# Sparse attention in a hybrid RWKV-7 and S5 model: top-256 keys by a bit search for the threshold, index scores computed one unit earlier, ties by a prefix sum

## The chip, the cores and the metric

The kernel runs on one core of a Trainium2 chip. A core has five engines with a queue each: PE (TensorE, matrix products), DVE (VectorE), ACT (ScalarE), POOL (GpSimd) and SP (SyncE, which here issues the DMAs). They run in parallel and wait for each other through semaphores. The metric is the device time of one execution in microseconds (us), the median of several runs.

## The reference

One program computes two blocks one after the other. The first is an RWKV-7 mixer and a short convolution; the change doesn't touch it. The second is a hybrid layer: an S5 state space branch with a gated unit, and a sparse attention. Only this part matters here:

```python
def block(args):                         # 128 queries at a time, 8 blocks
    blk, ql_b, qi_b, wi_b = args
    causal = key_pos[None, :] <= q_pos[:, None]
    idx_logits = jnp.einsum('bthd,bsd->bths', qi_b, ki)          # 8 index heads of 32
    index_score = jnp.einsum('bths,bth->bts', jax.nn.relu(idx_logits), wi_b)
    index_score = jnp.where(causal[None], index_score, neg)
    _, sel = lax.top_k(index_score, n_sel)                       # n_sel = 256 of 1024 keys
    ...
    s = jnp.einsum('bthc,btkc->bthk', ql_b, c_sel)               # 8 heads over a latent of 128
    s = jnp.where(valid[:, :, None, :], s, neg)
    p = jax.nn.softmax(s, axis=-1)
    return jnp.einsum('bthk,btkc->bthc', p, c_sel)
```

`top_k` takes, among equal scores, those with the lower index. The gated unit is `y = gelu(y); h = y @ w_glu + b_glu; val * sigmoid(gate)`, multiplied by `silu(gate_s)`, whose product with `w_in` is also made in that unit.

## The kernel before

All data are float32. After the first block, the second runs as four units, with a barrier of all engines at the end of each: the S5 scan with projections (lines 1486 to 1827), the gated unit (lines 1829 to 1944), attention (`attention_block`, line 1947) and the output product with layer norm (line 2290).

**The gated unit** has two loops. The first has 8 steps (j, `SUB`): GELU of 512 columns on ACT and DVE, four transposes on PE, a copy to `yT` on DVE (L1931), and beside it 8 matrix products of the gate (L1860) a step. The second has 4 steps (e, `NE`): 32 products of PE (L1889), two tanh on ACT, and five operations of DVE over 1024 columns (L1935 to L1943); PE's gate products for e+2 wait for DVE's L1940 (`out2`), and follow between the steps.

**Attention, preparation** (L1981 to L2058): index weights `wi` by a transpose, `kiT` (the index keys four times below each other) by four DMAs, `ql` and the latent `cT`. DVE ends with the gate's sigmoid (L2056, L2058), four times.

**Attention, main loop.** 8 blocks b of 128 queries, in each 8 heads h; a slot k is 8b+h. Block b sees `keys(b)` = 128(b+1) keys. In a slot PE makes the scores for slot k+2 (L2094), the transposes of the softmax (L2111), the values (L2119) and one product by `w_uv` (L2130); DVE adds the mask and takes the maximum (`softmax`, L2245 and L2248) and inverts the sum (L2266); ACT makes the exponentials and copies out of PSUM. Blocks 0 and 1 see at most 256 keys and need no choice.

Blocks 2 to 7 do. Before, in slots 0 to 47, PE also makes one head's index logits two blocks ahead (L2102), ACT takes the ReLU and the weight (L2185, L2194), POOL sums over heads (L2210) and DVE chooses for block b+1 in slots h = 1 to 7 of block b (`choose`): 32 rounds of the 8 largest by `max` (L2257) and their removal by `match_replace` (L2258), in place in `score`, then the mask `mb` (L2260).

```python
for i in range((h - 1) * steps // parts, h * steps // parts):
    ch(nc.vector.max(top[:, :], sc))
    ch(nc.vector.match_replace(sc, top[:, :], sc, LEAST))
```

`ch` makes DVE wait for its own last instruction. The order within each engine is written out by hand, nothing is scheduled by a tool.

## Time and profile before

| | |
|---|---|
| median of 3 runs | 4590.96 us (4587.19 to 4592.53) |
| the profiled execution's own time | 4586.48 us |
| its span, first to last instruction | 4584.8 us |
| busy: PE, DVE, ACT, POOL | 4219.0, 2370.4, 1315.9, 274.1 us |
| gated unit, first loop | from 3697 to 3749 us |
| gated unit, second loop | to 3857 us |
| attention, preparation | to 3889 us |
| attention, main loop | to 4442 us |
| output unit | to the end |

The stages follow one another in time. A share over the whole span says little on the change: what counts is which engine others wait for in the stages from 3697 to 4442 us.

### The profile page before, as it was taken

The page shows a single profiled execution, that of the slowest core. Times are in us where ns is not written, and L with a number is a line of the kernel's source. Part 1 is how long each engine was busy: PE and PEld are TensorE (multiplying, and loading weights), DVE is VectorE, ACT ScalarE, POOL GpSimd, SP SyncE. Part 2 cuts the span into 40 slices and gives each one's busy share as a digit, 9 for nine tenths or more (in the row PEclk, how much of TensorE's full clock was granted, in tenths as well). Part 3 has the DMA queues.
Part 4 walks back from the last instruction along what each step waited for, and adds up shares of the span by engine and source line. Part 5 has one row for each costly group of instructions (what it writes and reads, how often), then busy time and mean ns, then how long its engine had stood idle before and what let it go on. Part 6 is the DMA issues. An engine that isn't in the chain of part 4 may idle for free. (4 is left out here: it accounts for less than half of the span.)

```text
span 4584.8 us, 131580 instructions
## 1 busy us (share of the span) xinstructions
PE 4219.0 (92%) x58346; PEld 3217.2 (70%) x58346; DVE 2370.4 (52%) x5302; ACT 1315.9 (29%) x3044; POOL 274.1 (6%) x308
## 2 busy tenths in 40 slices
PE   7999999999999999998988999999969977877579
PEld 5888888888888888886777887888746643444344
DVE  4556555565555655554215543444255533688842
ACT  2233323332323223222213332232113312433221
POOL 1000000000000000000000000000000000111100
PEclk9999999999999999998999999999989988566789
DMA  2322222222222222221413333333211110000010
GB/s 74 92 68 79 63 88 68 83 64 78 77 79 68 79 68 77 70 79 50 127 37 110 96 96 83 101 96 96 55 42 28 23 37 9 1 1 0 0 46 37
DMA packets 520412, 289.54 MB, mean 63 GB/s; under 512 B 30256, under 2 KB 509728, under 8 KB 519904
## 3 DMA queue, kind: packets, MB, share of 16 engines
q1 hardware_dynamic: 519904, 281.88, 21.3%
q8 instruction: 427, 7.00, 0.6%
q14 instruction: 81, 0.66, 0.0%
HBM read 267.55 MB, written 12.58 MB: 61 GB/s over the span
## 5 line engine op out<-in xcount | busy, mean ns | idle before, releaser
L344 PE MATMUL a_bank<-a_lerps,a_wt 128*128 128x256 f32 x4096 | 1036.9, 393 | 2.4 <-DVE a_lerps L815 2.4
L344 PEld LDWEIGHTS a_bank<-a_lerps,a_wt 128*128 128x128 f32 x4096 | 731.0, 189 | 126.9 <-issue 21.2
L1208 PE MATMUL b_bank<-b_hR,b_wR 128*128 128x512 f32 x1024 | 399.8, 390 | 15.5 <-DVE b_wL L1213 15.5
L1208 PE MATMUL b_bank<-b_hL,b_wR 128*128 128x512 f32 x1024 | 399.7, 390 | 0.0
L1208 PE MATMUL b_bank<-b_hR,b_wL 128*128 128x512 f32 x1024 | 399.5, 390 | 0.0
L931 DVE TENSOR_TENSOR a_iv_X<-a_bank,a_iv_X 128x256 f32<-128x256 f32 x256 | 108.7, 425 | 413.3 <-PE a_bank L448 413.3
L1213 DVE TENSOR_TENSOR b_wL<-b_w,b_wR 128x1024 fp32r<-128x1024 f32 (+1 forms) x144 | 192.4, 1340 | 116.8 <-ACT b_wR L1296 104.0
L692 ACT ACTIVATE a_iv<-a_bank 128x512 f32<-128x512 f32 x192 | 114.7, 597 | 419.1 <-PE a_bank L454 266.2
L1208 PEld LDWEIGHTS b_bank<-b_hR,b_wR 128*128 128x128 f32 x1024 | 193.0, 188 | 56.0 <-issue 16.1
L1208 PEld LDWEIGHTS b_bank<-b_hL,b_wR 128*128 128x128 f32 x1024 | 192.9, 188 | 40.4
L1208 PEld LDWEIGHTS b_bank<-b_hR,b_wL 128*128 128x128 f32 x1024 | 193.0, 189 | 40.2
L1701 PE MATMUL s_proj<-xT,s_wp 128*128 128x512 f32 x384 | 172.3, 599 | 11.9 <-DMA s_wp<-in_w_in 11.9
L448 PEld LDWEIGHTS a_bank<-a_iv 32*32 32x32 f32 x12288 | 130.0, 105 | 70.1 <-issue 69.6
L2257 DVE MAX8 tb_top<-tb_score 128x8 f32<-128x384 f32 (+5 forms) x192 | 171.2, 892 | 5.2
L1008 DVE SCALAR_TENSOR_TENSOR a_S<-a_bank,a_scr,a_pr_H 128x64 f32<-128x64 f32 x256 | 72.5, 283 | 189.2 <-PE a_bank L568 189.2
L2258 DVE MATCH_REPLACE8 tb_score<-tb_top,tb_score 128x384 f32<-128x384 f32 (+5 forms) x192 | 168.1, 875 | 0.0
L1296 ACT ACTIVATE b_wR<-b_w 128x1024 fp32r<-128x1024 f32 x128 | 134.1, 1052 | 109.7 <-issue 90.5
L448 PE MATMUL a_bank<-a_iv 32*32 32x32 f32 x12288 | 157.5, 194 | 2.9 <-issue 2.7
L752 POOL TENSOR_TENSOR a_scr<-a_scr 128x256 f32<-128x256 f32 x64 | 46.5, 726 | 1760.3 <-ACT a_scr L658 1744.0
L2130 PE MATMUL t_po<-t_wuv,tb_oT 128*128 128x64 f32 x128 | 37.9, 394 | 107.8 <-ACT tb_oT L2191 101.5
L2119 PEld LDWEIGHTS t_po<-tb_pT,t_ck 128*128 128x128 f32 x576 | 97.6, 254 | 52.6 <-issue 49.2
L1701 PEld LDWEIGHTS s_proj<-xT,s_wp 128*128 128x128 f32 x384 | 71.3, 192 | 89.6 <-issue 89.6
(441 smaller groups left out, 8156.7 us busy)
## 6 DMA issues: line engine op xcount, KB each, us to landing
a_wt<-in_a_w_in SPq DMA_DIRECT2D x256, 512.0 KB, 4.2
b_w<-in_b_w_in SPq DMA_DIRECT2D x128, 512.0 KB, 4.0
b_w<-in_b_w_out SPq DMA_DIRECT2D x16, 1024.0 KB, 5.6
rwkv_out<-a_ybuf SPq DMA_DIRECT2D x64, 128.0 KB, 5.7
m_w<-in_a_w_out SPq DMA_DIRECT2D x16, 512.0 KB, 4.0
s_wp<-in_w_in SPq DMA_DIRECT2D x12, 512.0 KB, 3.8
a_xtok<-in_x SPq DMA_DIRECT2D x4, 1024.0 KB, 7.1
m_two<-rwkv_out SPq DMA_DIRECT2D x16, 256.0 KB, 3.0
```

The costliest lines, as they stand in the source:

```text
L344: r = mm(o, wt[:, j, c, :], src[:, c, :], start=(c == 0), stop=(c == ND - 1))
L448: r = mm(bank[bk][rows, at + c * CH:at + (c + 1) * CH][:, cols], lhs[rows, c, cols], rhs[rows, c, cols], start=True, stop=True)
L692: return a(tiles[:, :, :, :].rearrange("p w a b -> p (w a b)"), bank[bk][:, :], ACT.Copy, scale=scale).then_inc(s[done], 1)
L931: tt(x, bank[3][:, 0:PASS], x, ALU.add).then_inc(s[after], 1)
L1008: stt(S4[:, c + 1, :], bank[7][:, c * CH:(c + 1) * CH], e["eL"][:, (c + 1) * CH - 1:(c + 1) * CH], pr["H"][:, c, :], ALU.mult, ALU.add).th ...
L1208: m = nc.tensor.matmul(o, a, b, start=(first and i == 0), stop=(last and i == 2))
L1213: return eng.tensor_tensor(l, x, rounded.bitcast(F32), ALU.subtract)
L1296: nc.scalar.activation(wR[:, i, :, :], w[:, i, :, :], ACT.Copy).then_inc(s[f"wR{i}"], 1)
L1701: m = nc.tensor.matmul(proj[:, t], wp[i][:, c, :], xT[:, c, t], start=(c == 0), stop=(c == ND - 1))
L2119: m = nc.tensor.matmul(po[0][:, 0:P], ck[:, j, :], pT[k % 2][:, j * P:(j + 1) * P], start=(j == 0), stop=(j == k // AH))
L2257: ch(nc.vector.max(top[:, :], sc))
L2258: ch(nc.vector.match_replace(sc, top[:, :], sc, LEAST))
```

## The change

It has three parts.

1. **The index scores move.** `kiT`, `wi` and the logits are made in the first loop of the gated unit. The scores of blocks 2 to 7 are cut into 80 pieces (a block of up to 512 keys is one piece a head, the others two halves), 10 a step. For a piece PE makes one product, ACT the ReLU out of PSUM into one of four buffers, and DVE multiplies by the weight and adds (`weigh`), where ACT scaled and POOL added before. PSUM holds two pieces. POOL only applies the causal mask.
2. **The search.** A threshold for each query is found bit by bit: for each of 32 bits, count the scores of at least the candidate (`tensor_scalar` with a sum as second output), and set or clear the bit by two operations on 128x2 integers. Two blocks go through a bit together: group 0 is blocks 2 and 3 (384 and 512 keys), group 1 is 4 and 5 (640, 768), group 2 is 6 and 7 (896, 1024). Where the bits stand is a table:

```python
BITS_BEFORE = 8
BITS_AFTER = ([(0, i) for i in range(8, 23)], [(0, i) for i in range(23, 32)] + [(1, i) for i in range(0, 4)], [(1, i) for i in range(4, 10)], [])
BITS_PRELIM = range(10, 16)
BITS_1 = range(16, 32)
SLOT_2 = 12
```

So 8 bits stand between the gated unit's loops, 15, 13 and 6 after its steps e = 0, 1, 2, 6 of group 1 in the attention's preparation, the other 16 of group 1 one a slot in slots 0 to 15, and the 32 of group 2 one a slot in slots 12 to 43.
3. **The choice.** In slots h = 4, 5, 6 of block b, `choose(b+1)` counts what lies above the threshold, marks the equals, numbers them by a prefix sum, and keeps as many as there is room.

```diff
+    def bit(self, v, g, i):
+        if self.updated:
+            v.wait_ge(s["thr"], self.updated)
+        for b in GROUPS[g]:
+            if self.counted >= 2:
+                v.wait_ge(s["count"], self.counted - 1)
+            nc.vector.tensor_scalar(self.junk[self.counted % 2][:, 0:keys(b)], score_of(sel, b), sel["thr"][:, col].bitcast(F32), None,
+                                    ALU.is_ge, ALU.add, accum_out=sel["cnt"][:, col]).then_inc(s["count"], 1)
+            self.counted += 1
+        v.wait_ge(s["count"], self.counted)
+        place = 31 - i
+        nc.vector.tensor_scalar(sel["flip"][:, cols], sel["cnt"][:, cols], TOPK - 0.5, -1.0 if i == 0 else 2.0 ** place, ALU.is_lt, ALU.mult).then_inc(s["flip"], 1)
+        v.wait_ge(s["flip"], self.updated)
+        nc.vector.scalar_tensor_tensor(sel["thr"][:, cols], sel["flip"][:, cols], (1 << 30) if i == 0 else (1 << place) >> 1, sel["thr"][:, cols],
+                                       ALU.bitwise_xor, ALU.bitwise_xor).then_inc(s["thr"], 1)
...
                     for j in range(SUB):
+                        for n in range(j * PER, (j + 1) * PER):
+                            logits(n)
                         pe.wait_ge(s["gelu"], j + 1)
...
+                    def weigh(n):
+                        v.wait_ge(s["rl"], n + 1)
+                        if h == 0:
+                            ts(o, x, w, None, ALU.mult).then_inc(s["acc"], 1)
+                        else:
+                            v.wait_ge(s["acc"], before)
+                            stt(o, x, w, o, ALU.mult, ALU.add).then_inc(s["acc"], 1)
...
                     def choose(b, h):
-                        steps, parts = TOPK // 8, AH - 1
-                        for i in range((h - 1) * steps // parts, h * steps // parts):
-                            ch(nc.vector.max(top[:, :], sc))
-                            ch(nc.vector.match_replace(sc, top[:, :], sc, LEAST))
+                        if h == AH - 4:
+                            ch(ts(up, sc, t, None, ALU.is_gt, ALU.add, accum_out=above[:, i:i + 1]))
+                            ts(room[:, i:i + 1], above[:, i:i + 1], -UNIT, TOPK * UNIT, ALU.mult, ALU.add)
+                            ch(ts(eq, sc, t, UNIT, ALU.is_equal, ALU.mult))
+                        if h == AH - 3:
+                            ch(nc.vector.tensor_tensor_scan(up, eq, eq, 0.0, ALU.add, ALU.bypass))
+                            ch(stt(eq, up, room[:, i:i + 1], eq, ALU.is_le, ALU.mult))
+                        if h == AH - 2:
+                            ch(ts(out, sc, t, -UNIT, ALU.is_le, ALU.mult))
+                            ch(tt(out, out, eq, ALU.add))
...
-                        if k < ISLOTS:
-                            index(k)
```

In the gated unit, PE's first loop now reads as follows for its first two steps: `g_kiT` against `latent` are the index logits, `s_y` the transposes, `g_ws` the gate.

```order
L1944 MATMUL g_bank<-base_ident,latent 128x128 x8
L1952 MATMUL g_bank<-g_kiT,latent 128x384 x8
L1952 MATMUL g_bank<-g_kiT,latent 128x512 x2
L1964 MATMUL g_bank<-base_ident,s_y 128x128 x4
L1937 MATMUL g_bank<-xT,g_ws 128x512 x4
L1952 MATMUL g_bank<-g_kiT,latent 128x512 x6
L1952 MATMUL g_bank<-g_kiT,latent 128x320 x4
L1964 MATMUL g_bank<-base_ident,s_y 128x128 x4
L1937 MATMUL g_bank<-xT,g_ws 128x512 x4
```

The rows L1944 and L1952 are new there; before, transposes and gate products only alternated. On DVE the second step of the same loop reads now (`sel_score` holds the scores, `g_rl` the ReLU's buffers):

```order
L2049 TENSOR_SCALAR g_g<-g_g 128x512
L2050 TENSOR_TENSOR g_g<-g_g,s_y 128x512
L2043 SCALAR_TENSOR_TENSOR sel_score<-g_rl,g_wi,sel_score 128x512 x5
L2054 TENSOR_SCALAR g_g<-g_g 128x512
L2055 TENSOR_TENSOR s_y<-s_y,g_g 128x512
L2043 SCALAR_TENSOR_TENSOR sel_score<-g_rl,g_wi,sel_score 128x512
L2039 TENSOR_SCALAR sel_score<-g_rl,g_wi 128x320 x2
L2043 SCALAR_TENSOR_TENSOR sel_score<-g_rl,g_wi,sel_score 128x320 x2
L2059 COPY g_yT<-g_bank 128x512
```

Ten operations, L2043 and L2039, stand between the five that a step had before. In the attention loop, one slot of block 4 on DVE before, from one reciprocal to the next (ISA is the masked maximum and its read-out):

```order
L2266 RECIPROCAL tb_den<-tb_den 128x1
L2245 ISA tb_sm,tb_mx<-t_big,tb_mb 128x640
L2245 ISA tb_mx 128x1
L2248 TENSOR_SCALAR tb_nmx<-tb_mx 128x1
L2257 MAX tb_top<-tb_score 128x8
L2258 MATCH_REPLACE tb_score<-tb_top,tb_score 128x768
L2257 MAX tb_top<-tb_score 128x8
L2258 MATCH_REPLACE tb_score<-tb_top,tb_score 128x768
```

and so on for four or five pairs. The same block in the changed kernel, a slot with h = 5 (`sel_thr` the threshold, `tb_same` the equals):

```order
L2345 RECIPROCAL tb_den<-tb_den 128x1
L2319 ISA tb_sm,tb_mx<-t_big,tb_mb 128x640
L2319 ISA tb_mx 128x1
L2322 TENSOR_SCALAR tb_nmx<-tb_mx 128x1
L1524 TENSOR_SCALAR t_junk,sel_cnt<-sel_score,sel_thr 128x896
L1524 TENSOR_SCALAR t_junk,sel_cnt<-sel_score,sel_thr 128x1024
L1531 TENSOR_SCALAR sel_flip<-sel_cnt 128x2
L1533 SCALAR_TENSOR_TENSOR sel_thr<-sel_flip,sel_thr 128x2
L2336 SCALAR_TENSOR_TENSOR tb_upto<-tb_same 128x768
L2337 SCALAR_TENSOR_TENSOR tb_same<-tb_upto,tb_room,tb_same 128x768
```

The pairs are gone; one bit of group 2 (L1524 to L1533) stands in the slot, and here a third of the choice (L2336, the prefix sum, and L2337).

## Rows read from the trace of the kernel before

**Rows 1.** Windows: a piece of the gated unit's first loop; attention loop; blocks 2, 4, 6, 7

```profile
core 0: us, PE busy (x) PEld busy (x) DVE busy (x) ACT busy (x) POOL busy (x), PEclk, DMA share, GB/s
...
3720.00:3748.00 28.00, 24.58 (x73) 10.98 (x72) 17.95 (x28) 5.83 (x11) 0.00 (x0) 1.00 0.00 1
...
3889.00:4442.00 553.00, 409.28 (x1376) 252.98 (x1376) 425.74 (x846) 188.95 (x416) 77.80 (x58) 0.65 0.00 1
...
3984.00:4046.00 62.00, 51.96 (x129) 29.76 (x128) 54.07 (x130) 21.41 (x52) 11.78 (x9) 0.50 0.00 1
...
4125.00:4211.00 86.00, 64.80 (x214) 40.08 (x213) 73.39 (x130) 30.81 (x58) 15.82 (x9) 0.68 0.00 0
...
4305.00:4402.00 97.00, 46.51 (x197) 33.38 (x196) 91.34 (x127) 16.99 (x36) 0.00 (x0) 0.72 0.00 0
...
4409.00:4442.00 33.00, 29.64 (x200) 24.05 (x200) 8.04 (x25) 16.80 (x34) 0.00 (x0) 1.00 0.00 1
```

**Rows 2.** Groups of instructions, whole run: the old search, count | busy us, mean ns | idle before

```profile
L2257 DVE MAX8 tb_top<-tb_score 128x8 f32<-128x384 f32 (+5 forms) x192 | 171.2, 892 | 5.2
...
L2258 DVE MATCH_REPLACE8 tb_score<-tb_top,tb_score 128x384 f32<-128x384 f32 (+5 forms) x192 | 168.1, 875 | 0.0
```

**Rows 3.** Timeline of DVE, one slot of block 4: start us, us

```profile
4155.75 0.16 DVE L2266 RECIPROCAL tb_den<-tb_den 128x1 f32<-128x1 f32 x1
...
4156.95 0.15 DVE L2248 TENSOR_SCALAR tb_nmx<-tb_mx 128x1 f32<-128x1 f32 x1
...
4157.02 0.95 DVE L2257 MAX8 tb_top<-tb_score 128x8 f32<-128x768 f32 x1
...
4167.26 0.16 DVE L2266 RECIPROCAL tb_den<-tb_den 128x1 f32<-128x1 f32 x1
```

**Rows 4.** Groups by shape, DVE, whole run: mean ns of one

```profile
L2361 DVE TENSOR_SCALAR o_r<-o_r,o_st 128x1024 f32<-128x1024 f32 x8 | 6.5, 812 | 0.3
...
L2260 DVE TENSOR_SCALAR tb_mb<-tb_score 128x1024 f32<-128x1024 f32 x1 | 0.7, 693 | 0.0
...
L2260 DVE TENSOR_SCALAR tb_mb<-tb_score 128x384 f32<-128x384 f32 x1 | 0.4, 359 | 0.0
...
L2245 DVE CUSTOM_DVE_ANT_0 tb_sm<-t_big,tb_mb 128x1024 f32<-128x1024 f32 x8 | 9.8, 1225 | 20.1 <-PE t_big L2094 19.9 <-DVE tb_den L2266 0.2
...
L826 DVE TENSOR_TENSOR_SCAN a_scr<-a_const_chunk_keep,a_scr 128x256 f32<-128x256 f32 x64 | 44.3, 692 | 2.2
...
L1384 DVE TENSOR_SCALAR b_tap<-b_cols 128x3 f32 x30 | 35.0, 1165 | 0.0
...
L2052 DVE SCALAR_TENSOR_TENSOR t_cT<-latent,tp_kvg,tp_rs 128x1024 f32<-128x1024 f32 x1 | 1.3, 1285 | 0.0
```

**Rows 5.** Timeline, one step of the gated unit's first loop

```profile
3740.67 1.08 DVE L1931 COPY g_yT<-g_bank 128x512 f32<-128x512 f32 x1 [0.75 <-PE g_bank L1871]
...
3745.13 3.60 PE L1860 MATMUL g_bank<-xT,g_ws 128*128 128x512 f32 x8
...
3745.33 1.08 DVE L1931 COPY g_yT<-g_bank 128x512 f32<-128x512 f32 x1 [0.75 <-PE g_bank L1871]
```

**Rows 6.** Timeline of DVE, second loop of the gated unit, with idle before

```profile
3763.64 0.69 DVE L1935 TENSOR_SCALAR g_th<-g_th 128x1024 f32<-128x1024 f32 x1 [17.23 <-ACT g_th L1908]
...
3799.46 0.69 DVE L1935 TENSOR_SCALAR g_th<-g_th 128x1024 f32<-128x1024 f32 x1 [30.69 <-ACT g_th L1908]
...
3834.45 0.69 DVE L1935 TENSOR_SCALAR g_th<-g_th 128x1024 f32<-128x1024 f32 x1 [29.85 <-ACT g_th L1908]
...
3851.70 0.69 DVE L1935 TENSOR_SCALAR g_th<-g_th 128x1024 f32<-128x1024 f32 x1 [12.12 <-ACT g_th L1908]
```

**Rows 7.** Timeline of DVE, the attention unit's preparation

```profile
3881.25 0.69 DVE L2056 TENSOR_SCALAR tp_gt<-tp_gt 128x1024 f32<-128x1024 f32 x1 [5.61 <-ACT tp_gt L2035]
```

**Rows 8.** Timeline of PE, block 7: transposes of two slots in a row

```profile
4417.85 1.04 PE L2111 MATMUL t_tp<-base_ident,tb_sm 128*128 128x128 f32 x8
...
4422.45 1.04 PE L2111 MATMUL t_tp<-base_ident,tb_sm 128*128 128x128 f32 x8
```

More of the change, by code:

```diff
@@ L1845, in s5_block, with halves, last_piece @@
             sg = sb("sg", [P, SEQ])
+            kiT = sb("kiT", [P, SEQ])
+            wi = sb("wi", [P, NB, IH])
+            rl = sb("rl", [P, 4, HALF])
+            qiT = latent[:, 1:3, :]
+            def halves(b):
+                parts = 1 if keys(b) <= HALF else 2
+                return [slice(i * keys(b) // parts, (i + 1) * keys(b) // parts) for i in range(parts)]
+            pieces = [(b, h, t) for b in range(B0, NB) for h in range(IH) for t in halves(b)]
+            PER = len(pieces) // SUB
+            def last_piece(b):
+                return max(n for n, piece in enumerate(pieces) if piece[0] == b)
             with nc.Block() as block:
@@ L1960, in attention_block @@
         NQ = AH * AD // P
-        qT, qiT = mixed[:, 0:NQ, :], latent[:, 1:3, :]
-        kiT = sb("kiT", [P, SEQ])
-        wi = sb("wi", [P, NB, IH])
+        qT = mixed[:, 0:NQ, :]
+        junk = [sb(f"junk{i}", [P, SEQ]) for i in range(2)]
+        search = Search(nc, s, sel, junk)
         cT = sb("cT", [P, SEQ])
@@ L2065, in sb3 @@
                 return sub.enter_context(nc.sbuf_tensor("tb_" + name, shape, dt))
-            rl = [sb3(f"rl{i}", [P, SEQ]) for i in range(2)]
-            score = [sb3(f"score{i}", [P, SEQ]) for i in range(2)]
-            top = sb3("top", [P, 8])
+            same, upto = sb3("same", [P, SEQ]), sb3("upto", [P, SEQ])
+            above, room = sb3("above", [P, NI]), sb3("room", [P, NI])
             mb = [sb3(f"mb{i}", [P, SEQ]) for i in range(2)]
@@ L2095, in scores @@
                         m.then_inc(s["sc"], 1)
-                    def index(k):
-                        b, h = divmod(k, IH)
-                        pe.wait_ge(s["pT"], k + 1)
-                        rows = slice((h % 4) * IDIM, (h % 4 + 1) * IDIM)
-                        for t in pieces(keys(b + B0)):
-                            m = nc.tensor.matmul(tp[:, t], qiT[rows, h // 4, (b + B0) * P:(b + B0 + 1) * P], kiT[rows, t], start=True, stop=True)
-                        m.then_inc(s["logit"], 1)
                     def turn(k):
```

167 lines of the change are left out of this document (100 added, 67 removed).

## The prediction

> **What bounds the kernel now.** The page shows PE busy for most of the span, but that is the RWKV and convolution part, which stays as it is. I cut the rest into its stages by the timeline and read the windows. In the attention loop DVE is busy 425.7 of 553 us, in block 4 it is 73.4 of 86 us and in block 6 91.3 of 97, while PE's granted clock averages 0.65 over the loop and 0.50 in block 2 [rows 1]. The groups name DVE's work: MAX8 and MATCH_REPLACE8, 192 of each, 171.2 and 168.1 us [rows 2]. The timeline of one slot shows it as a chain: from the reciprocal at 4155.75 the softmax part takes until 4157.02, that is 1.27 us, and the next reciprocal comes at 4167.26, a slot of 11.5 us, filled with five pairs without gaps [rows 3]. Block 7 has no choice to make and shows the loop without it: PE's transposes come 4.60 us apart [rows 8], at a granted clock of 1.0 and with PE 29.6 of 33 us busy [rows 1]. So the loop is bound by DVE in blocks 1 to 6 and by PE in block 7. In the gated unit's first loop a step is 4.66 us, from copy to copy [rows 5], PE is busy 24.6 of 28 us and DVE 17.95 [rows 1], thus DVE has 3.0 us of work in each step, 3.2 with its gaps. In the second loop DVE waits 17.2, 30.7, 29.9 and 12.1 us ahead of its four steps [rows 6]; that is cover, of nearly 90 us.
>
> **The price of the new operations.** Times of DVE go by two rates. A `tensor_scalar` over SBUF takes 693 ns for 1024 elements and 359 ns for 384, that is 0.52 ns an element over some 0.16 us; one with two column operands takes 812 ns. The masked maximum, which also writes out an accumulated value, takes 1225 ns for 1024, or 1.04 ns an element [rows 4]. No row shows a `tensor_scalar` that also sums. Its bounds are therefore 0.69 and 1.23 us for 1024, and as a far one 2.08 ns an element, the prefix sum's rate (692 ns for 256, less 0.16) [rows 4]. I take 1.04 ns an element, because the operation nearest in what it does, an elementwise operation with an accumulator read out behind it, has that rate. A column operand adds 0.06 us (1285 against 1225 ns) [rows 4], an accumulator's read-out with its gap about 0.05. A 128x1 operation takes 0.15 us [rows 3], with its gap 0.19. So one bit, two counts and two small operations, costs:
> group 0 (384, 512 keys): 0.56 + 0.69 + 0.12 + 0.10 + 0.39 = 1.86 us;
> group 1 (640, 768): 0.83 + 0.96 + 0.61 = 2.39 us;
> group 2 (896, 1024): 1.09 + 1.23 + 0.61 = 2.93 us.
> All 96 bits are 230 us, against 339 for the pairs, and 42 of them now stand in DVE's waits of the second loop.
>
> The Trainium skill, "VectorE: DVE Perf Modes", section "The perf-mode tier table (the rule you actually need)", gives `tensor_scalar` in fp32 two elements a cycle in SBUF and doesn't say what an accumulator changes. The 693 ns row agrees for the plain form. By that rule for the counts as well, the case "half-priced counts" below would hold.
>
> **First loop of the gated unit: +43 us.** DVE gets 80 pieces, 33.8 thousand elements in all (8 heads times 4224 keys). At 1.04 ns they are 35.2 us, with 80 times 0.22 us fixed 52.8; the 10 first ones of each head's kind run at the fast rate, -2.2; and 80 gaps of 0.04 make 3.2: 53.8 us. With the 8 steps of 3.2 us this is 79 us of DVE, 9.9 a step, so DVE becomes the bound, not PE (per step 3.6 for the gate's 8 instructions, and for ten products, at the same 0.45 us for 512 columns and 422 columns on the mean, 3.7 [rows 5]). The start costs about 5 us: eight transposes, `wi`, four DMAs of `kiT`, a first product and ReLU come ahead of the first piece; PE's old wait for the DMA of `ws` goes under it. Between a step's last product and the next step's first stand transposes and gate, some 4 us of PE at full clock, with some 5 us of DVE work as cover (pieces still in the buffers, copy, first GELU part). That is near, and I allow 1 us a step, 8 in all. Sum 92 us, against 49: +43. Bounds: +35 with no such stall, and at half clock the gate takes 3.6 us more a step, 29 in all, which gives +72. POOL's last mask (0.3 us) and a semaphore come behind.
>
> **Second loop: +3 us.** The 8 bits take 14.9 us with 0.8 ahead of them, in a wait of 17.2 us which the last pieces shorten: about 1 us late. After e = 0, 15 bits are 27.9 of 30.7 us. After e = 1, 9 and 4 bits are 26.3 of 29.9. After e = 2, 6 bits of group 1 are 14.3 against 12.1 [rows 6]: 2 us late. What is late then is DVE's L1935, which holds the unit's end.
>
> **Attention, preparation: +9 us.** 6 bits, 14.3 us, stand ahead of DVE's gate operations, which waited 5.6 us for ACT's tanh [rows 7]. ACT's tanh and PE's start of the main loop are held by them. The transposes, DMAs and scaling that left this unit lay beside the wait for `w_uk` and the reciprocal, and give nothing.
>
> **Main loop: -245 us.** Index products, ReLU, scaling and POOL's sums leave it. DVE's slot is 1.27 us at 640 keys [rows 3], so 0.60 + 1.04 n, n in thousands of keys: 0.73 in block 0 to 1.67 in block 7. `choose` is 6.25 n + 1.5 (two operations at the fast rate, three at 1.04, the prefix sum at 2.08 ns): 4.0 us for block 2, 8.0 for block 7. PE's slot is 4.6 us at full clock in block 7 and taken in proportion to b + 1, twice that at half clock. The blocks:
> 0: 8 times (0.73 + 2.39) = 25. 1: 7 + 0.7 (the gated product) + 4 slots of one bit, 9.6, + 4 of both groups, 21.3, + 4 = 42.5. 2: 8 + 0.7 + 23.4 + 4.8 = 37, with PE 28 at half clock: 38. 3: 38.7, PE 37 at half clock: 41. 4: 40.7, but PE 46 at half clock and 23 at full: 46. 5: four slots with bits, 11.2 + 0.7 + 11.7 + 7.2 = 31; PE 28 or 55: 39. 6: DVE 21, PE 32 at full clock, and the slots h = 4 and 5 of DVE are longer than PE's: 37. 7: 38. With 2 us at the start 308, against 553.
> I take full clock in blocks 6 and 7, because block 7 before has it as soon as no choice holds its PE, and a mixture in 4 and 5. Blocks 0 to 3 are DVE's at either clock.
>
> **Sum.** 43 + 3 + 9 - 245 = -190 us. From the profiled execution's 4586.48 that is 4396, from the median, which is 4.5 us above it, **4401 us**.
>
> **The rivals.**
> *Half-priced counts.* The sum comes at no cost and the counts run at 0.52 ns an element. Bits are then 1.48, 1.74 and 2.0 us with column operands at the higher price. The second loop is not late (3 less), the preparation is +5 (4 less), and the main loop 20, 33, 31, 36, 42, 36, 37, 38 = 273 (35 less): 4359 us. For it speaks the 693 ns row; against it that every row with an accumulator on DVE has the other rate.
> *PE stays at half clock.* Before, it did in blocks 0 to 2 with PE 52 of 62 us busy [rows 1]. If so to the end, the blocks are 25, 43, 38, 41, 48, 55, 64, 74 = 388, 80 more, and the gated unit's gate 29 more: 4510 us. Against it stands block 7.
> *The small operations are dear.* This one ends on the other side. L1384, three elements in a `tensor_scalar`, takes 1165 ns [rows 4] where others of its size take 150; it has a variable address and I see no other reason. The 192 operations on 128x2 integers are of a kind that no row shows. At 1165 ns each they would add 194 us, with little cover left, and give 4595. From 0.99 us each on the change loses.
> *Slow counts*, at the prefix sum's rate: 32 times 4224 elements times 1.04 ns, +141 less some 10 of cover: 4530 us.
> *The scores' part costs more than it gives:* a stall at each piece (PSUM holds two) would add 0.3 us to each of 80 pieces, +24, 4425; it lies in the range.
>
> **How the numbers follow.** Forecast 0.60, half-priced counts 0.25, half clock 0.06, small operations 0.03, slow counts 0.03, others 0.03. The first two have their middles at 4401 and 4359; to both go the first loop's bounds (-8, +29), and the clock in blocks 4 to 6 (-15 at full, +45 at half, seldom all). So 4345 to 4460; the forecast's own range is 4380 to 4460. A measurement of this kernel tells a change of 0.2%, 9 us. Faster 0.95, within it 0.01, slower 0.04 (the small operations and part of the others).
>
> **What would show it.** Counts of 1024 keys at 1.2 to 1.3 us (or 0.7 to 0.85 for the rival); a gated first loop of some 92 us with DVE busy over 85%; `thr` operations at 0.15 to 0.2 us; in blocks 1 to 4 slots that end on DVE, at 4.6 to 5.3 us; blocks 6 and 7 at clock 1.0 with slots near 4 to 5 us; an attention loop of about 308 us. I am wrong if the first loop is beyond 120 us, or if the clock in blocks 6 and 7 is near 0.5.

## The result and the profile after

The kernel after takes 4417.38 us (median of 4 runs, 4416.63 to 4417.93), the kernel before in the same session 4589.07 us (4 runs, 4586.53 to 4592.53). The ratio is 0.9625, with a 95% interval from 0.9609 to 0.9642: 3.75% faster. The forecast was 4401 us with a range from 4345 to 4460. The sum was off by 16 us, and two of its terms by more than that, in opposite directions: the good total is in part luck.

The stages, cut at the same places in both traces: the gated unit's first DMA and scaling, the first product of its second loop, its last product into `mixed`, attention's first masked maximum, the last gated product. Times are in us.

| stage | before | after | change | forecast |
|---|---|---|---|---|
| up to the gated unit (not touched) | 3697.0 | 3702.5 | +5.5 | 0 |
| gated unit, first loop | 51.6 | 136.9 | +85.3 | +43 |
| gated unit, second loop | 107.0 | 108.3 | +1.3 | +3 |
| attention, preparation | 34.4 | 41.8 | +7.4 | +9 |
| attention, main loop | 551.8 | 283.4 | -268.4 | -245 |
| output | 143.0 | 143.2 | +0.2 | 0 |

The first row is a difference in parts that are the same in both. It differs by this much from run to run: the experiments below, in which these parts are the same too, start the gated unit between 3693 and 3701 us. So stages are compared below by their own length.

The windows of the kernel after answer to [rows 1]: the whole first loop, four pieces of it within two steps, and attention's blocks 1 to 7.

```profile
core 0: us, PE busy (x) PEld busy (x) DVE busy (x) ACT busy (x) POOL busy (x), PEclk, DMA share, GB/s
3702.00:3840.00 138.00, 132.38 (x267) 55.43 (x268) 77.73 (x137) 52.05 (x98) 1.76 (x6) 0.69 0.10 35
...
3756.00:3762.00 6.00, 6.00 (x17) 2.25 (x15) 2.84 (x6) 3.24 (x7) 0.29 (x1) 1.00 0.00 0
3763.00:3768.00 5.00, 5.00 (x11) 2.17 (x10) 3.65 (x7) 1.99 (x4) 0.00 (x0) 0.50 0.00 0
3769.00:3775.00 6.00, 6.00 (x16) 2.37 (x15) 1.94 (x4) 1.96 (x4) 0.00 (x0) 1.00 0.00 0
3776.00:3785.00 9.00, 9.00 (x16) 4.17 (x17) 6.11 (x11) 3.21 (x7) 0.29 (x1) 0.50 0.00 0
...
4018.00:4060.00 42.00, 23.41 (x88) 18.30 (x88) 38.20 (x114) 11.12 (x39) 0.00 (x0) 0.63 0.00 1
4060.00:4096.00 36.00, 24.13 (x112) 17.90 (x112) 33.13 (x90) 13.15 (x41) 0.00 (x0) 0.81 0.00 1
4096.00:4133.00 37.00, 27.03 (x142) 20.29 (x142) 34.72 (x90) 14.35 (x41) 0.00 (x0) 0.86 0.00 1
4133.00:4172.00 39.00, 30.53 (x176) 24.11 (x176) 36.30 (x89) 15.91 (x40) 0.00 (x0) 0.91 0.00 1
4172.00:4205.00 33.00, 30.63 (x201) 24.82 (x200) 25.72 (x60) 18.80 (x42) 0.00 (x0) 1.00 0.01 1
4205.00:4240.00 35.00, 34.19 (x224) 27.39 (x224) 19.28 (x42) 19.84 (x41) 0.00 (x0) 1.00 0.00 1
4240.00:4273.00 33.00, 29.64 (x200) 24.05 (x200) 8.03 (x25) 16.86 (x34) 0.00 (x0) 1.00 0.00 1
```

Two things are to be seen. In the first loop it is PE that is busy, 132.4 of 138 us, and DVE only 77.7; I had forecast the reverse. Its clock averages 0.69 there, and the mean hides two levels: within one step it is 1.0, then 0.50, then 1.0 again, with PE busy throughout. In the attention loop DVE is nearly full in blocks 1 to 4 and PE in 5 to 7, and the clock is at 0.81 as early as block 2, where before it was at 0.50 [rows 1].

The chain of work in one step of the first loop, by the timeline of the kernel after (PE, ACT and DVE):

```profile
3756.81 9.04 PE L1952 MATMUL g_bank<-g_kiT,latent 32*128 32x320 f32 x20
...
3763.66 1.10 ACT L1997 ACTIVATE g_rl<-g_bank 128x384 f32<-128x384 f32 x2 [1.12 <-PE g_bank L1952]
...
3766.68 4.70 PE L1937 MATMUL g_bank<-xT,g_ws 128*128 128x512 f32 x8
...
3771.32 10.03 PE L1952 MATMUL g_bank<-g_kiT,latent 32*128 32x384 f32 x20
3772.26 0.49 ACT L1997 ACTIVATE g_rl<-g_bank 128x384 f32<-128x384 f32 x1 [5.37 <-PE g_bank L1952]
3772.78 1.26 DVE L2043 SCALAR_TENSOR_TENSOR sel_score<-g_rl,g_wi,sel_score 128x384 f32<-128x384 f32 x2 [3.79 <-ACT g_rl L1997]
```

The ten index products of a step are twenty matmul instructions (x20). ACT waits for PE and DVE for ACT. The clock is 1.0 when the index products begin at 3756.8, falls during them at 3762, and comes back at about 3769, some 2 us into the eight gate instructions.

DVE's operations by shape, in the kernel after, answer to [rows 4]:

```profile
L1524 DVE TENSOR_SCALAR_CACHE_REDUCE t_junk<-sel_score,sel_thr 128x1024 f32<-128x1024 f32 x32 | 40.8, 1275 | 0.0
...
L1531 DVE TENSOR_SCALAR sel_flip<-sel_cnt 128x2 int32<-128x2 f32 x96 | 16.3, 169 | 3.3
...
L1533 DVE SCALAR_TENSOR_TENSOR sel_thr<-sel_flip,sel_thr 128x2 int32<-128x2 int32 x96 | 15.5, 161 | 3.3
...
L1524 DVE DVE_READ_ACCUMULATOR t_junk<-sel_score,sel_thr 128x1 f32 x108 | 9.0, 83 | 0.0
...
L2336 DVE TENSOR_TENSOR_SCAN tb_upto<-tb_same 128x1024 f32<-128x1024 f32 x1 | 2.3, 2281 | 0.0
```

A count of 1024 keys is 1275 ns, as forecast (1.23 and 0.06), and the small operations are 169 and 161 ns. DVE's waits in the second loop, by its timeline, answer to [rows 6]; what was 17.2, 30.7, 29.9 and 12.1 us is now 4.6, 5.0, 5.5 and nothing:

```profile
3854.48 0.70 DVE L2068 TENSOR_SCALAR g_th<-g_th 128x1024 f32<-128x1024 f32 x1 [4.58 <-ACT g_th L2015]
...
3890.32 0.69 DVE L2068 TENSOR_SCALAR g_th<-g_th 128x1024 f32<-128x1024 f32 x1 [5.00 <-ACT g_th L2015]
...
3925.32 0.70 DVE L2068 TENSOR_SCALAR g_th<-g_th 128x1024 f32<-128x1024 f32 x1 [5.47 <-ACT g_th L2015]
...
3943.78 0.69 DVE L2068 TENSOR_SCALAR g_th<-g_th 128x1024 f32<-128x1024 f32 x1
```

### The profile page after: what moved, and what is told of

It is laid out like the page before. It is cut to its first block and busy times, and to the rows that moved or that the text cites. A ratio compares the mean times of both kernels' runs of the same rounds, so it can differ in the third digit from the quotient of the medians.

```text
span 4416.1 us, 131760 instructions
## 1 busy us (share of the span) xinstructions
PE 4128.5 (93%) x58346; PEld 3176.2 (72%) x58346; DVE 2300.1 (52%) x5425; ACT 1287.6 (29%) x3028; POOL 198.9 (5%) x260
## 5 line engine op out<-in xcount | busy, mean ns | idle before, releaser
L1208 PE MATMUL b_bank<-b_hR,b_wR 128*128 128x512 f32 x1024 | 399.9, 390 | 15.5 <-DVE b_wL L1213 15.5
L1095 PE MATMUL m_bank<-m_yR,m_wR 128*128 128x512 f32 x256 | 108.1, 422 | 19.3 <-DVE m_yL L1048 16.9
L1000 DVE TENSOR_TENSOR a_pr_G<-a_const_diag,a_bank 128x256 f32<-128x256 f32 x64 | 27.0, 421 | 187.7 <-PE a_bank L436 187.7
L2412 PE MATMUL o_bank<-o_wo,mixed 128*128 128x512 f32 x256 | 115.9, 606 | 5.4 <-DMA o_wo<-in_w_out 5.3
L1208 PE MATMUL b_bank<-b_yR,b_wR 128*128 128x512 f32 x256 | 101.6, 397 | 15.2 <-DVE b_wL L1213 15.2
```

The lines of the kernel that those rows point to most:

```text
L1095: r = nc.tensor.matmul(o[:, :], a[i][:, c, :], b[:, kq * ND + c, tokens(h)], start=(kq == 0 and c == 0 and q == 0), stop=False)
L1208: m = nc.tensor.matmul(o, a, b, start=(first and i == 0), stop=(last and i == 2))
L2412: nc.tensor.matmul(bank[b % 2][:, t], mixed[:, k, tb], wo[:, k, t], start=(k == 0), stop=False)
```

## The experiments

The first loop was the open question, with three theories at first. A: PE's own work bounds it, because a product is two instructions. B: PE and ReLU wait for each other at the two places in PSUM. C: the block of gate products between two steps starves ReLU and DVE. After the first four runs two more came up: D, that products which use only 32 of the array's 128 rows let PE's clock fall, and E, that PE's waits do. Their stage times, from the traces, in us, are in this table. "Whole" is the kernel's own time, a median where it says how many runs, otherwise one run. "Half columns" and "plain counts" leave a part of the work out, so their results are not the program's, and their times only measure what was left out.

| kernel | first loop | second loop | preparation | main loop | whole |
|---|---|---|---|---|---|
| after | 136.9 | 108.3 | 41.8 | 283.4 | 4417.4 (4 runs) |
| gate spread | 197.0 | 110.0 | 41.7 | 282.7 | 4475.0 (4 runs) |
| four places | 123.1 | 107.7 | 42.1 | 283.7 | 4402.6 |
| half columns | 112.9 | 108.3 | 41.8 | 283.4 | 4390.2 |
| plain counts | 137.0 | 107.1 | 38.2 | 243.0 | 4369.6 |
| full rows | 104.8 | 107.2 | 42.3 | 282.5 | 4381.5 (4 runs) |
| full rows, gate spread | 103.3 | 108.6 | 42.3 | 284.0 | 4376.1 |
| full rows, four places | 99.9 | 107.8 | 41.8 | 283.5 | 4376.0 |
| early bits | 137.0 | 106.9 | 35.5 | 263.3 | 4385.7 (4 runs) |
| full rows, early bits | 123.7 | 108.8 | 35.4 | 263.3 | 4375.2 |
| together | 102.4 | 107.7 | 35.4 | 273.8 | 4365.6 (5 runs) |
| together, first step in a block | 99.2 | 107.6 | 35.5 | 273.8 | 4363.0 (5 runs) |

### Gate products spread between the index products

```diff
                         for n in range(j * PER, (j + 1) * PER):
                             logits(n)
+                            i = n - j * PER
...
+                            if i % 2 and i < 8:
+                                gate(j // (SUB // 2), range(j % 4 * 4 + i // 2, j % 4 * 4 + i // 2 + 1))
...
-                        gate(j // (SUB // 2), range(j % 4 * 4, j % 4 * 4 + 4))
```

> The four gate products of a step of the gated unit's first loop (8 matmul instructions) no longer stand in a row behind the transposes, but one by one behind the index products 1, 3, 5 and 7 of the step. Nothing is left out; PE has the same work. In the changed kernel that loop takes 136.9 us, PE is busy 132.4 of 138. Theory A (PE's own work bounds the loop; twenty index matmul instructions a step where I had counted ten): the loop can give back only the small waits for ReLU, now filled by gate products: 125 to 134 us, whole kernel 3 to 12 us less (4405 to 4414). Theory C (the block of gate products between two steps starves ReLU and DVE, which waits 4.5 us at each step's start): seven such waits go, the loop falls to 100 to 107 us, whole kernel 30 to 37 us less (4380 to 4387).

Measured: 4474.95 us (4472.94 to 4476.59), ratio to before 0.9751 (0.9735 to 0.9767). The loop took 197.0 us, 60 more. Both theories had it shorter, and both were wrong. The windows of this kernel over the loop, and PE's weight loads in one stretch of it:

```profile
3697.00:3894.00 197.00, 188.70 (x266) 65.68 (x267) 74.90 (x127) 52.38 (x98) 1.75 (x6) 0.50 0.07 24
```

```profile
3798.34 0.50 PEld L1952 LDWEIGHTS g_bank<-g_kiT,latent 32*128 32x128 f32 x2 [1.50 <-issue]
3799.15 0.33 PEld L1952 LDWEIGHTS g_bank<-g_kiT,latent 32*128 32x128 f32 x1 [0.31 <-issue]
3799.79 0.33 PEld L1952 LDWEIGHTS g_bank<-g_kiT,latent 32*128 32x128 f32 x1 [0.31 <-issue]
3801.20 0.50 PEld L1937 LDWEIGHTS g_bank<-xT,g_ws 128*128 128x128 f32 x2 [1.08 <-issue]
3803.20 0.50 PEld L1952 LDWEIGHTS g_bank<-g_kiT,latent 32*128 32x128 f32 x2 [1.50 <-issue]
```

The clock is 0.50 for the whole loop, though PE is busy 188.7 of 197 us and has the same instructions as in the kernel after. So it is not waiting of PE that holds the clock down here. There is a smaller second cost. At this clock an index instruction of 384 columns starts 0.64 us after the one before (3799.15 to 3799.79). Four of them would be 2.56 us; the gate's load comes 2.86 us after the first (3798.34 to 3801.20). Going from one kind of product to the other thus costs 0.3 us, 64 times in the loop, some 19 us. The rest, about 40, is put down to the clock by this difference.

### Four places in PSUM

```diff
-                        if n >= 2:
+                        if 4 <= n < DEEP:                 # DEEP = 40
+                            pe.wait_ge(s["rl"], n - 3)
+                        if n >= DEEP:
                             pe.wait_ge(s["rl"], n - 1)
```

The places alternate over the two first banks and both halves of the fourth, which the gate uses from step 4 on.

> The index products of the first 40 of 80 pieces (steps 0 to 3 of the first loop) have four places in PSUM in turn, not two; the rest has two as before. Nothing is left out. Steps 0 to 3 take about 65 us in the changed kernel. Theory A (PE's work bounds): a piece of 384 columns came 0.75 us after the one before where its two matmul instructions are about 0.64 us, so at most 0.1 us of each of 40 pieces goes: steps 0 to 3 2 to 5 us shorter. Theory B (two places make PE and ReLU wait for each other, which is what stretched the loop): 0.4 us or more a piece, steps 0 to 3 at least 15 us shorter. Theory C (gate block): no change in either.

Measured: 4402.57 us, one run. The loop is 13.8 us shorter, between the bounds of A and B. The steps, from copy to copy, are 13.8, 11.6, 10.8 and 14.0 us, against 15.6, 14.2, 15.4 and 15.5; after that they are alike. In the step of 10.8 us the clock averages 0.82 and in that of 15.4 us 0.72, because the twenty index instructions then take 4.8 us and are over before the clock falls.

A third effect is in this run, which none of the theories had. With four places PE has two index products under way at once. Consecutive heads stand in different groups of 32 rows, and their instructions overlap in time. These are the twenty index instructions of two steps in this kernel, by PE's timeline:

```profile
3734.94 4.50 PE L1962 MATMUL g_bank<-g_kiT,latent 32*128 32x320 f32 x20
...
3745.57 4.82 PE L1962 MATMUL g_bank<-g_kiT,latent 32*128 32x320 f32 x20
```

The kernel with full rows and four places below has the same twenty instructions on 128 rows, at the same clock of 1.0. There they come one after another and take 5.54 us for the first of these steps and 6.40 for the second (from 3738.70 to the end of the last row):

```profile
3738.70 1.24 PE L1964 MATMUL g_bank<-g_kz,latent 128*128 128x320 f32 x4
3739.78 1.45 PE L1964 MATMUL g_bank<-g_th,latent 128*128 128x384 f32 x4
3741.07 1.45 PE L1964 MATMUL g_bank<-g_sg,latent 128*128 128x384 f32 x4
3742.36 2.74 PE L1964 MATMUL g_bank<-g_kz,latent 128*128 128x384 f32 x8
```

So the 14 us are the places' own, the overlap's and the clock's, and this run doesn't part them. The full-row kernels below tell only the places' own.

### Half the columns

```diff
+                        w = (t.stop - t.start) // 2 if n >= 2 else HALF
```

with the product written into `HALF:HALF + w` from the keys `t.start:t.start + w`.

> Each index product from the third piece on is made for the first half of its columns only; ReLU and DVE still take all columns, so half of the index scores are left out (old PSUM contents stand in their place) and the keys chosen are others. PE's index instructions go from 81.2 us to about 41 us or somewhat more. Theory A (PE's work bounds): the first loop falls by 30 to 40 us, from 136.9 to 97 to 107, DVE's 78 us of work are the next bound. Theory B (handing over between PE and ReLU): the products' latency is half of each turn, so the loop falls by 10 to 20 us. Theory C (gate block between the steps): as B or less, and DVE's waits of 4.5 us at each step's start stay whole.

Measured: 4390.18 us, one run; the loop is 24.0 us shorter, between A's 30 to 40 and B's 10 to 20. PE's index instructions fell from 81.2 to 50.8 us, by 30.4, and the loop by most of that. So PE's work bounds the loop for the most part, and C, which had as much as B or less, doesn't explain it. But 81.2 us for 160 instructions is itself the number that the clock makes.

### Plain counts

```diff
             nc.vector.tensor_scalar(self.junk[...], score_of(sel, b), sel["thr"][:, col].bitcast(F32), None,
-                                    ALU.is_ge, ALU.add, accum_out=sel["cnt"][:, col])
+                                    ALU.is_ge)
...
```

> The counts are plain comparisons without the summed output, the count is a constant; the search is left without its result (the threshold comes out near 2, so hardly a key of blocks 2 to 7 is chosen). Same number of instructions on DVE. My reading: the summed output is what makes a count of 1024 keys 1275 ns; the plain one takes 0.69 to 0.76 us and 512 keys 0.43 to 0.50, and no 83 ns read-out follows. The second loop's bits lie under waits, so DVE's waits there grow and the loop gains 0 to 3 us; the preparation 3 to 4 us; the main loop, bound by DVE in blocks 1 to 4 and by PE in 5 to 7, 20 to 35 us; whole kernel 4380 to 4393. Rival (the rate comes from the column operand or from fp32 comparisons, not from the sum): counts stay at 1.2 to 1.3 us, and the time within 3 us of the changed kernel's.

Measured: 4369.55 us, one run, with this group of counts by shape:

```profile
L1524 DVE TENSOR_SCALAR t_junk<-sel_score,sel_thr 128x1024 f32<-128x1024 f32 x32 | 23.9, 748 | 0.0
```

The same operation on the same column operand takes 748 ns without the sum and 1275 with it, and 83 more for the read-out. So it is the sum that has the lower rate, and the rival is wrong. The second loop gained 1.2 us and the preparation 3.6, as said; the main loop gained 40.4, more than the 35 at the top of my range, in blocks 0 to 5, and so the whole kernel came out 10 us under the 4380 to 4393 expected. The Trainium skill ("VectorE: DVE Perf Modes", section "The perf-mode tier table (the rule you actually need)") gives `tensor_scalar` in fp32 two elements a cycle; the 748 ns row agrees for the plain form, and the 1275 ns row shows that the form with a summed output doesn't have it.

### Full rows

The index products get a stationary operand of all 128 rows, four heads at once, and keys that are zero outside the rows of one head.

```diff
-            kiT = sb("kiT", [P, SEQ])
+            kz = [th, sg] + [sb(f"kz{i}", [P, SEQ]) for i in range(2)]      # zeros, then 32 rows by DMA
...
-                        nc.tensor.matmul(bank[...], qiT[rows, h // 4, b * P:(b + 1) * P], kiT[rows, t], ...)
+                        nc.tensor.matmul(bank[...], qiT[:, h // 4, b * P:(b + 1) * P], kz[h % 4][:, t], ...)
```

> The index products use all 128 rows of TensorE: instead of one tile of keys repeated in four groups of 32 rows there are four tiles, each with the keys in its own 32 rows and zeros in the others. Same number of instructions and columns, same results; added are four memsets ahead of the DMAs (1 to 3 us). In the changed kernel the granted clock falls to 0.50 about 6 us into each step's index products (32 rows) and comes back 2 to 3 us into the gate products (128 rows); the loop takes 136.9 us at a mean of 0.69. Theory D (products on 32 rows let the clock fall): the clock stays at 1.0 from the first gate products on, PE's step is 7.0 for index products, 3.5 gate and 1 transposes, 11.5 us, with waits for ReLU 12: the loop takes 105 to 115 us, whole kernel 4385 to 4397. Rival E (the waits of PE for ReLU between the products let it fall): the clock stays at a mean near 0.7 and the loop at 135 to 142 us, whole kernel 4415 to 4423.

Measured: 4381.46 us (4378.10 to 4383.98), ratio 0.9548 (0.9532 to 0.9564), 36 us under the kernel after. The loop took 104.8 us, at the lower edge of theory D's 105 to 115, and the whole kernel 3.5 us less than its 4385 to 4397. The windows of this kernel, over the loop and over one early and one late step:

```profile
3699.00:3804.00 105.00, 99.35 (x265) 44.42 (x266) 75.54 (x131) 52.30 (x98) 3.81 (x8) 0.95 0.13 46
...
3730.00:3741.00 11.00, 10.96 (x35) 5.28 (x34) 8.56 (x17) 5.54 (x13) 0.00 (x0) 1.00 0.01 2
...
3776.00:3789.00 13.00, 13.00 (x35) 5.27 (x34) 9.81 (x17) 6.68 (x12) 0.29 (x1) 1.00 0.01 2
```

The clock is 1.00 from the second step on and 0.95 over the loop; what is left at 0.50 lies at the start. PE's weight loads still waited for ReLU 62 times, against 60 in the kernel after, so rival E (the waits) is wrong for this loop. That 96 of the rows multiply zeros doesn't matter to the clock.

Two limits of this reading. The edit changes two things: how many rows a product uses, and that heads took turns on four groups of 32 rows and now all use the same 128. No run separates these. And fewer than 128 rows don't lower the clock everywhere. The first block of this program, which the change doesn't touch, has thousands of products on 64 and 32 rows between those on 128. These are two of its windows in the kernel before, the second one with products on 64 rows alone, which start in pairs some 7 ns apart:

```profile
100.00:2140.00 2040.00, 2035.94 (x48680) 1667.98 (x48676) 1127.75 (x3151) 622.34 (x1843) 130.23 (x151) 1.00 0.25 74
622.20:627.90 5.70, 5.70 (x149) 5.37 (x148) 3.69 (x13) 2.04 (x11) 1.84 (x2) 1.00 0.33 95
```

The clock is 1.00 there. So what is shown is the fall of this stream of index products, 32 rows at a time and mostly one after another, and not a rule for small products.

With the gate products spread as well, by the diff of the first experiment:

> As the full-row kernel, and the four gate products of a step stand between the index products, as in the spread kernel, whose loop took 197 us at a clock of 0.50 throughout. Same results. Theory D (32 rows let the clock fall): the clock is at 1.0, the loop takes 100 to 110 us, no longer than the full-row kernel's, because the gate products now fill PE's waits for ReLU. Rival F (alternating the two kinds of product is what holds the clock down or costs a drain of 0.3 us each time, whatever their rows): the clock stays at 0.50 or the loop is over 20 us longer than the full-row kernel's.

Measured: 4376.08 us, one run; loop 103.3 us, where the same order with 32 rows took 197.0. Theory D holds and rival F falls. From step 1 on a step is 0.6 to 1.3 us shorter than with the gate in a block; that is all that C's starving is worth here, seven times 1 us and not the 30 to 37 us that it had promised. So C is out. The first step is 6 us longer (its first copy comes 25.1 us after the start, against 19.1). The 0.3 us between kinds of product is gone too. In the kernel called "together" in the table two gate instructions of 512 columns are followed by the index products after 0.86 us, twice the 0.43 of such an instruction (PE's timeline):

```profile
3712.98 2.07 PE L1949 MATMUL g_bank<-xT,g_ws 128*128 128x512 f32 x2 [3.49 <-DMA g_ws<-in_w_in]
...
3716.65 1.02 PE L1949 MATMUL g_bank<-xT,g_ws 128*128 128x512 f32 x2
3717.51 0.81 PE L1965 MATMUL g_bank<-g_th,latent 128*128 128x384 f32 x2
```

With four places in PSUM as well, by the diff of the second:

> As the full-row kernel, and four places in PSUM for the first 40 index products, as in the kernel with four places (loop 123.1 us, of which steps 0 to 3 took 14 us less than with two, partly because the clock fell later). Same results. If PE's waits for ReLU cost 0.1 us a piece and the clock is at 1.0 in both, steps 0 to 3 are 4 to 6 us shorter than in the full-row kernel and steps 4 to 7 the same: loop 100 to 110 us. If the clock doesn't stay up on full rows, the loop takes 120 to 125 us as with 32 rows.

Measured: 4376.04 us, one run; loop 99.9 us, 4.9 less than with two places, nearly all of it in steps 1 to 4. That is what two places cost at full clock where products come one after another, 0.12 us for each of 40 pieces. Of the 13.8 us of the kernel with four places and 32 rows about 9 are therefore the clock's and the overlap's together; no run separates them.

### The same edit in the kernel before

```diff
-                            m = nc.tensor.matmul(tp[:, t], qiT[rows, h // 4, ...], kiT[rows, t], start=True, stop=True)
+                            m = nc.tensor.matmul(tp[:, t], qiT[:, h // 4, ...], kz[h % 4][:, t], start=True, stop=True)
```

> The kernel before the change with the one edit of the full-row kernel: its index products, which stand in the attention loop's slots, use 128 rows with zeros in 96 of them, and four memsets precede the DMAs; same results. The loop took 554 us with the granted clock at 0.50 in block 2, 0.65 to 0.69 in blocks 3 to 5, DVE busy 80 to 94% of blocks 2 to 6. Theory D (products on 32 rows let the clock fall): the clock of blocks 3 to 5 rises to 0.85 or more; since DVE bounds these blocks, the time falls by 0 to 15 us only (4574 to 4590). Rival E (PE's idle time lets it fall there, and rows don't matter): clocks within 0.05 of before, time within 4 us of 4589.

Measured: 4576.51 us (8 runs, 4573.39 to 4578.62), ratio 0.9975 (0.9964 to 0.9985). The windows of attention's block 0, first of the kernel before and then of this one, and of its block 2, which answers to [rows 1]:

```profile
3890.00:3929.00 39.00, 38.03 (x90) 20.18 (x89) 6.05 (x42) 19.68 (x66) 8.44 (x11) 0.50 0.00 1
```

```profile
3892.00:3919.00 27.00, 21.90 (x90) 14.17 (x89) 6.43 (x42) 18.75 (x67) 8.53 (x12) 0.88 0.00 1
...
3972.00:4034.00 62.00, 36.48 (x130) 22.52 (x128) 54.10 (x130) 21.72 (x53) 11.78 (x9) 0.79 0.00 1
```

Block 0, the one block with index products in which DVE had next to nothing to do, went from 39 to 27 us and makes up the whole kernel's gain of 11 us. In the others DVE is the bound and the time stays within 2 us, as expected; there the clock went from 0.50 to 0.79 in block 2 and from 0.67 to 0.69 up to 0.77 and 0.78 in blocks 3 to 5. I had expected 0.85 or more, so rows are not all of it: PE's idle time may have the rest; in the kernel before it was 10 us in block 2 and 21 in block 4 [rows 1]. The Trainium skill ("TensorE: Matmul & The Clock Gate", section "HAM oscillation — how this bites in real kernels") puts such falls down to PE's waits for data. That may hold for the rest here, which no run separates; it doesn't hold for the gated unit's loop with the gate spread, where the clock was 0.50 with PE busy 188.7 of 197 us.

### Early bits, and the findings together

```diff
+BITS_LOOP = [[], [], [0, 1, 2, 3], [4, 5, 6, 7], [8, 9, 10, 11], [12, 13, 14, 15], [16, 17, 18, 19], [20, 21]]
...
+                        bits_of(BITS_LOOP[j][:2])         # ahead of the second GELU part
                         v.wait_ge(s["th"], j + 1)
...
                         nc.vector.tensor_copy(yT[:, :, j::SUB], ...)
+                        bits_of(BITS_LOOP[j][2:])
```

> Only the places of the search's bits change: 22 of the first group's 32 bits stand in steps 2 to 7 of the gated unit's first loop (four a step, two behind the copy and two ahead of the second GELU part), the other 10 ahead of the second loop's first step, 29 bits of the second group in the second loop and 3 in the preparation; no bit of the second group is left for attention's first 16 slots. Same results. Theory (DVE idles 59 us in the first loop because PE bounds it): 22 bits at 1.8 us are 39 us of work in these waits, 4.6 to 7 us a step, so the loop grows by at most 10 us; the preparation gives back 3 times 2.25, 7 us; attention's blocks 0 and 1 give back 16 bits, of which PE's own pace takes part: 20 to 30 us. Whole kernel 4380 to 4400. Rival (DVE work in the loop delays ReLU through the four score buffers, and PE behind it, so that each of the bits costs there what it saves later): loop 25 to 40 us longer, whole kernel 4410 to 4425.

Measured: 4385.71 us (4383.62 to 4387.20), ratio 0.9559 (0.9543 to 0.9575). The loop stayed at 137.0 us with 22 bits more in it and DVE busy 108.4 us instead of 77.7. They were free: PE is the bound there, and the rival, with 25 to 40 us, is wrong. The preparation gave back 6.3 us and the main loop 20.1.

> Full-row index products (loop 104.8 us) and the 22 early bits (loop 137.0 us where PE bounded it at a mean clock of 0.69, attention 263.3) in one kernel, two PSUM places, gate in a block; same results. If the early bits were free only because PE was slow: DVE has 9.2 us of old work and 7.2 of bits a step, the loop is DVE's at 15 to 17 us a step with bits, 128 to 138 us in all, and the kernel is within 10 us of the early-bits kernel's 4386. Rival (the bits fit in either case): loop near 112 us, whole kernel 4350 to 4362.

Measured: 4375.15 us, one run. The loop took 123.7 us, between the 128 to 138 and the 112 expected, and the whole kernel fell between them too: on full rows the 22 bits cost 18.9 us, 0.86 each. Both edits fill the same idle time of DVE, the one by shortening it and the other by working in it, so together they gain 42 us where each alone gains 36 and 32.

The kernel with everything together has this table of bits beside the edits named:

```diff
+BITS_LOOP = [[], [], [0], [1], [2], [3], [4], [5]]
...
-BITS_PRELIM = range(10, 16)
-BITS_1 = range(16, 32)
-SLOT_2 = 12
+BITS_PRELIM = range(19, 22)
+BITS_1 = range(22, 32)
+SLOT_2 = 10
```

> The findings together, with the same results: index products on 128 rows; gate products between them; four places in PSUM for the first 32; one bit of the first group in each of steps 2 to 7 of the first loop, 26 bits of it and 19 of the second group in the second loop, 3 in the preparation, 10 in attention's slots 0 to 9, the third group in slots 10 to 41. If DVE bounds the first loop now (8.3 to 10.4 us of work a step, and 1.8 for the bit), it takes 95 to 103 us; the preparation and the second loop stay within 1 us of the early-bits kernel's 35.5 and 106.9; six bits fewer in attention's slots are 7 to 9 us off 283.4. Whole kernel 4355 to 4366. Rival (DVE has no room left in the first loop, each bit costs its 1.8 us and delays ReLU as well): loop 110 us or more, whole kernel 4368 to 4378, no better than the full-row kernels at 4376.

Measured: 4365.60 us (4362.33 to 4370.79), ratio 0.9515 (0.9502 to 0.9528). The first loop is within the expectation at 102.4 us, and so is the whole. Its first copy comes late, 24.4 us after the start: the row at 3712.98 above shows PE waiting 3.49 us for the gate's weights, with index products behind the waiting one. The last run takes that away, with the first step's gate in a block as in the kernel after:

```diff
-                            if i % 2 and i < 8:
+                            if j and i % 2 and i < 8:
...
                         if j == 0:
                             pe.wait_ge(s["ws"], 16)
+                            gate(0, range(4))
```

> As the kernel that puts the findings together (4365.6 us, first loop 102.4), but the first step keeps its four gate products in a block behind the transposes; from the second step on they stand between the index products. Same results. In the kernel of before this edit PE waited at 3712.98 for the DMA of the gate's weights with the index products behind it, and the first copy came 24.4 us after the start, where it came at 19.1 with the block. If that wait is all, the first loop takes 96 to 98 us and the whole kernel 4358 to 4362. Rival (the loop's sum is DVE's work, so an earlier start is lost again in the later steps): 101 to 103 us and 4364 to 4367.

Measured: 4362.95 us (4359.76 to 4363.73), ratio 0.9508 (0.9495 to 0.9521). The first copy comes at 19.1 us again, but the step after it is 12.8 us where it was 10.7, so 3.2 of the 5.3 us remained: 99.2 us, between the two expectations. It is the fastest of these kernels, 1.2% under the kernel after; the difference to the one before it, 2.6 us, is no more than single runs scatter (8.5 us in that one's five).

## Why the prediction was right, and where it was not

**The main mechanism** was right. DVE's pairs bounded attention, a bit costs what was forecast or a little less, and its bits take the place of 339 us of pairs [rows 2]. Both prices of which the rivals were made came out on the forecast's side: the counts have the rate of an operation with an accumulator (1275 against 748 ns), and the small operations cost 0.16 us, not 1.2. Had the counts been plain, the stages would be 45 us shorter (1.2, 3.6 and 40.4), and the rival's 42 was about its size. One figure of the rivals is wrong by its own sum: small operations at 1165 ns each give 4595, so the change loses from about 1.14 us each on; 0.99 is what may be added to the 0.15.

**First loop, +43 forecast, +85 measured.** The step that failed is the one that made DVE the bound: "for ten products, at the same 0.45 us for 512 columns and 422 columns on the mean, 3.7". The 0.45 us [rows 5] is the time of one instruction, and the row's "x8" are the instructions of four products. I took the gate's eight instructions whole, and then counted one instruction for each index product where there are two. Twenty instructions are about 7 us at full clock instead of 3.7, a step of PE is over 11 us, and DVE's 9.9 of my sum is no longer the bound. This mistake and the waits at two PSUM places are 10 us of the 42 (the loop on full rows takes 104.8 us, my sum had 94.6 by the same cut, which has 51.6 for the loop of before where I wrote 49). The other 32 us came with the products on 32 rows, and most of them are the clock: at 0.3 us or less each, the two changes between kinds of product in a step are 5 us at most. My upper bound had half clock for the gate alone, 72 us of growth, and so left out the products that pull the clock down. The prediction's own sign of being wrong, a first loop beyond 120 us, came true with 137.

**Second loop and preparation**, +3 and +9, came out at +1.3 and +7.4: a bit of the second group took 2.25 us where I had 2.39. The covers were read rightly, except that the eight bits ahead of the loop's first wait are not late but leave 4.6 us of it.

**Main loop, -245 forecast, -268.4 measured.** Blocks 1 to 3, between gated products, are 41.9, 35.9 and 37.1 us against 42.5, 38 and 41. Block 4 is 39.5 against 46, 5 is 32.6 against 39, 6 is 35.1 against 37. Block 7 is 33.2 against 38; it is 33.2 in the kernel before as well (the window of [rows 1] has 33), so eight slots of 4.6 us each were too much for it. What was mis-sized most is the mixture of clocks taken for blocks 4 and 5, 13 us of the 23: they ran at 0.91 and 1.00, and block 4 at DVE's own pace (40.7 in my sum). I had read the low clock of before as a property of the loop's waits. A part of it belonged to the index products, which the change takes away: in the kernel before with full rows block 2 has 0.79 for 0.50, but block 4 only 0.78 for 0.68. What lifted block 4 further to 0.91 no run shows. So a cause that I had not seen made the first loop some 32 us too short in my sum, which the full rows show, and may have had a share in the 13 us by which blocks 4 and 5 were too long, which is argued from the clocks and not shown apart. The errors cancelled in part by luck, and the total was nearer than its parts deserved.

**PSUM stall, put at 0.3 us a piece** in the rival inside the range, is 0.12 at full clock.

Not tried: how many rows of the index products are enough to keep the clock, whether it is their number or the turns between groups of rows that counts, whether 32-row products would do as well with all of them overlapping, and what holds the clock below 1.0 in the blocks that DVE bounds.

## What to carry to other kernels

Count instructions of a product from a row with its x and the number of products in the code, for each product kind that a sum uses; a factor of two there moves the bound to another engine. When work moves from one stage to another, ask what it does to TensorE's clock in both: read the granted clock in pieces of a few us, not as a mean over the stage, and look which product stands where it falls. Where a product's contraction is short and the products come one after another, try padding it with zero rows: it cost the products nothing here (0.43 us for an instruction of 512 columns either way at full clock) and brought 32 us by the clock. It gives up the overlap of products in different groups of rows, which was worth 1.0 and 1.6 us in the two steps shown above. And before idle time of an engine is called lost, see whether other work can be put into it, as the 22 bits were at no cost.

## What the runs showed of the hardware

- Index products on 32 of 128 rows, mostly one after another: the granted clock fell from 1.0 to 0.50 during them with PE busy throughout, and came back during products on 128 rows; alternating both kinds held it at 0.50 for 197 us. With 128 rows, 96 of them zeros, it stayed at 1.00 (loop 136.9 to 104.8 us), and alternating was free (103.3 us). In the first block it stayed at 1.00 during a stretch of 64-row products that start in pairs (5.7 us with PE busy throughout).
- Index products in different groups of 32 rows overlap when PSUM has four places: twenty instructions took 4.50 and 4.82 us, against 5.54 and 6.40 on 128 rows, all at full clock.
- Changing between products on 32 and on 128 rows cost 0.3 us each time at the half clock; between two kinds on 128 rows nothing at the full.
- A `tensor_scalar` in fp32 over 1024 elements with a column operand takes 748 ns, with a summed output 1275 ns and 83 ns for the read-out. The prefix sum over 1024 takes 2281 ns.
- Two PSUM places for products of 0.64 us and a ReLU of 0.49 us cost 0.12 us a piece against four, at full clock and on 128 rows.
